# Activation-table loads, first copies and one transposition group moved within a two-block transformer kernel

## What is computed

```
h = rmsnorm(x, g_mix_pre); proj = h @ w_in
y = concat(rmsnorm(forgetting_attention(...)), rmsnorm(chunked_relpos_attention(...)))
x = x + rmsnorm(y @ w_out)
x = x + rmsnorm(memory_cross_attention(rmsnorm(x), rmsnorm(mem), ...))
x = x + rmsnorm(square(relu(rmsnorm(x) @ w_ff1)) @ w_ff2)
proj = rms_norm(x) @ w_in_2            # second block
o_gdn = gated_delta_rule(...) ; o_att = dsa_sparse_attention(...)
x = x + (sigmoid(ga) * o_gdn + sigmoid(gb) * o_att) @ w_out_2
x = x + square(relu(rms_norm(x) @ w_mlp_up)) @ w_mlp_down
```

## Time and profile before

| | |
|---|---|
| median of three runs | 921.76 us |
| the profiled execution | 921.96 us |
| its span | 920.1 us |
| TensorE (matmul) busy | 897.4 us, 98% |
| VectorE busy | 575.2 us, 63% |
| ScalarE busy | 511.8 us, 56% |
| GpSimd busy | 89.6 us, 10% |
| loaded from memory | 147.99 MB |

### The profile page before, as it was taken

The page is one execution under the profiler, slowest core; times in us unless marked ns, Lnnn a source line. Parts: engine busy times, 40 slices in busy tenths (PEclk is TensorE's granted clock), DMA queues, the critical chain, the costliest instruction groups (busy, mean ns, idle before and its releaser), DMA issues.

```text
span 920.1 us, 14611 instructions
## 1 busy us (share of the span) xinstructions
PE 897.4 (98%) x5672; PEld 797.0 (87%) x5672; DVE 575.2 (63%) x899; ACT 511.8 (56%) x932; POOL 89.6 (10%) x111
## 2 busy tenths in 40 slices
PE   6999999999999999999999999999999999999998
PEld 6998977888899998887778989988899799998886
DVE  5455656664676664445656998889846676665333
ACT  4466666664665554335557668787255465554330
POOL 0010000000000000001000412241152101000000
PEclk9999999999999999999999999999999999999999
DMA  9756333464455566555364544454430456555552
GB/s 341 254 183 230 107 124 108 148 226 92 146 175 184 183 207 185 195 202 195 107 214 138 184 139 141 134 164 157 99 143 1 131 190 184 184 183 183 184 189 84
DMA packets 110395, 152.22 MB, mean 165 GB/s; under 512 B 6752, under 2 KB 68344, under 8 KB 109944
## 3 DMA queue, kind: packets, MB, share of 16 engines
q1 hardware_dynamic: 110328, 151.31, 50.7%
HBM read 147.99 MB, written 3.30 MB: 164 GB/s over the span
## 4 chain that ended last, share of the span: by engine, by line
issue 48%; PE 34%; DVE 9%; ACT 4%; POOL 2%; DVEq 1%; DMA 1%; POOLq 1%; ACTq 0%; SPq 0%
PE acc L455 4%; PE acc L469 4%; PE acc L467 4%; PE acc L468 4%; PE acc L457 4%; PE acc L456 4%; DVE s_w_lo L405 3%; ACT s_w_hi L399 1%; PE acc L495 1%; DVE s_qkvT L1522 1%; PE acc L497 1%; PE acc L496 1%; DMA s_w_raw<-in_w_out 1%; ACT s_relu_i L1445 1%; POOL s_rstd L636 1%
## 5 line engine op out<-in xcount | busy, mean ns | idle before, releaser
L405 DVE TENSOR_TENSOR s_w_lo<-s_w_raw,s_w_hi 128x2048 fp32r<-128x2048 f32 (+1 forms) x198 | 312.2, 1594 | 176.5 <-ACT s_w_hi L399 176.2
L399 ACT ACTIVATE s_w_hi<-s_w_raw 128x2048 fp32r<-128x2048 f32 (+1 forms) x198 | 262.7, 1345 | 148.6 <-PE acc L457 102.3
L467 PE MATMUL acc<-s_h_hi,s_w_hi 128*128 128x256 f32 x800 | 229.1, 286 | 0.8 <-DVE s_h_lo L690 0.8
L469 PE MATMUL acc<-s_h_hi,s_w_lo 128*128 128x256 f32 x800 | 227.3, 284 | 0.0
L468 PE MATMUL acc<-s_h_lo,s_w_hi 128*128 128x256 f32 x800 | 227.3, 284 | 0.0
L467 PEld LDWEIGHTS acc<-s_h_hi,s_w_hi 128*128 128x128 f32 x800 | 154.5, 193 | 1.6 <-issue 1.2
L468 PEld LDWEIGHTS acc<-s_h_lo,s_w_hi 128*128 128x128 f32 x800 | 154.6, 193 | 0.3
L469 PEld LDWEIGHTS acc<-s_h_hi,s_w_lo 128*128 128x128 f32 x800 | 154.4, 193 | 0.0
L457 PE MATMUL acc<-s_w_hi,s_hid_lo 128*128 128x512 f32 x224 | 88.3, 394 | 0.0
L456 PE MATMUL acc<-s_w_lo,s_hid_hi 128*128 128x512 f32 x224 | 87.8, 392 | 0.0
L455 PE MATMUL acc<-s_w_hi,s_hid_hi 128*128 128x512 f32 x224 | 86.9, 388 | 0.0
(11 more groups left out here) (323 smaller groups left out, 1429.1 us busy)
## 6 DMA issues: line engine op xcount, KB each, us to landing
s_w_raw<-in_w_in SPq DMA_DIRECT2D x43, 1024.0 KB, 5.2
s_w_raw<-in_w_ff SPq DMA_DIRECT2D x32, 1024.0 KB, 5.2
s_w_raw<-in_w_mlp_up SPq DMA_DIRECT2D x16, 1024.0 KB, 5.5
s_w_raw<-in_w_mlp_down SPq DMA_DIRECT2D x16, 1024.0 KB, 5.0
s_w_raw<-in_w_out SPq DMA_DIRECT2D x8, 1024.0 KB, 5.1
s_w_raw<-in_w_mk SPq DMA_DIRECT2D x4, 1024.0 KB, 5.4
s_w_raw<-in_w_mv SPq DMA_DIRECT2D x4, 1024.0 KB, 5.0
s_w_raw<-in_w_mq SPq DMA_DIRECT2D x4, 1024.0 KB, 5.0
```

What stands on the lines that cost most here:

```text
L399: act.activation(w_hi[u % SPLIT_SLOTS][:, cs], w_raw[u % RAW_SLOTS][:, cs], ACT.Copy).then_inc(w_hi_done, 4 if q is None else 1)
L405: dve.tensor_tensor(w_lo[u % RAW_SLOTS][:, cs], w_raw[u % RAW_SLOTS][:, cs], w_hi[u % SPLIT_SLOTS][:, cs].bitcast(F32), ALU.subtract).then ...
L467: pe.matmul(o, wh[:, cs], hi[:, k, :], start=k == 0, stop=False)
L469: i = pe.matmul(o, wl[:, cs], hi[:, k, :], start=False, stop=k == KC - 1)
```

## The change

Five edits, all of them of the order of work; one new tile of one column and one new activation, used twice.

1. At the start, ScalarE splits quarters 0 and 1 of the first unit, copies banks 0 and 1 to h_hi, splits quarters 2 and 3, and copies banks 2 and 3.
2. Ahead of the evacuation of the second cv unit, ScalarE runs an exponential of one column into the tile `spare`.
3. The gate's activations of the second block stand one unit earlier: behind the first iq unit and no longer behind the first aq unit.
4. Ahead of the evacuation of the second aq unit, the exponential of one column again.
5. Of the five transposition groups behind k = 5, the fifth (the keys) stands behind k = 6, on TensorE and on ScalarE.

```diff
+        spare = sb("spare", [P, 1])
...
-        def nt_act(act, n, hi):
-            for j in range(4):
+        def nt_act(act, n, hi, banks=range(4)):
+            for j in banks:
...
+        def exp_table(act):
+
+            act.activation(spare[:], minus1[:], ACT.Exp)
...
-        def aqk_pe(pe):
-            for j in range(5):
+        def aqk_pe(pe, groups):
+            for j in groups:
...
-        def aqk_act(act):
-            for j in range(5):
+        def aqk_act(act, groups):
+            for j in groups:
...
-            for q in range(4):
+            for q in (0, 1):
                 unit_hi(act, 0, q)
             act.wait_ge(gain_in, 16)
-            nt_act(act, "mix", h_hi)
+            nt_act(act, "mix", h_hi, (0, 1))
+            for q in (2, 3):
+                unit_hi(act, 0, q)
+            nt_act(act, "mix", h_hi, (2, 3))
...
-            for j in range(2):
-                act_unit(act, "cv", j)
+            act_unit(act, "cv", 0)
+            advance_hi(act, of["cv"][1])
+            exp_table(act)
+            evacuate(act, "cv", 1)
...
             act_unit(act, "iq", 0)
+            gates2_act(act)
             act_unit(act, "iq", 1)
             ik_act(act)
             act_unit(act, "aq", 0)
-            gates2_act(act)
             idx_tr_act(act)
-            act_unit(act, "aq", 1)
+            advance_hi(act, of["aq"][1])
+            exp_table(act)
+            evacuate(act, "aq", 1)
             gates2_act_eg(act)
...
                 if k == 5:
-                    aqk_act(act)
+                    aqk_act(act, range(4))
+                if k == 6:
+                    aqk_act(act, (4,))
...
                 if k == 5:
-                    aqk_pe(pe)
+                    aqk_pe(pe, range(4))
+                if k == 6:
+                    aqk_pe(pe, (4,))
```

## The result

The kernel after took 925.13 us (median of ten executions, 923.31 to 925.42), the kernel before 922.4 us beside it (921.55 to 922.78). The ratio is 1.0027, 95% interval 1.0019 to 1.0035: slower by about 2.5 us, where 2.6 us of gain were forecast. The profiled execution of after took 925.12 us, with a span of 923.3 us.

What follows compares the result with a forecast made beforehand. TensorE, busy 897.4 of 920.1 us, was taken as the bound, so only its waits could be won. 0.30 + 1.04 + 0.43 + 0.86 + 0 = 2.63 us gave 919.1 us; stated range 918.0 to 921.3, from part bounds 918.5 to 920.2.

Steps and rivals of the forecast that it cites:

- The 0.08 us added to each idle: Each printed TensorE idle was priced 0.08 us higher, halfway between 0 and 0.16, because matmuls overlap.
- no row prices that, and I take 0: The new 4-byte tile shifts later tiles' addresses; taken as 0 us because all transfers keep their sizes.
- Part 1: Start: earlier h_hi copies let TensorE start 0.59 us earlier, of which 0.30 us is kept, bounds 0 and 0.6.
- the cap: Fourth unit, 31.39: its weights' landing time stays, so TensorE can be at most 0.3 us earlier from there.
- Part 2: First attention: earlier exponential table load removes the 0.96 us wait at the transposes; 1.04 us, bounds 0.9 and 1.1.
- Part 3: Gate: activations one unit earlier remove the 0.35 us wait of its transposes; 0.43 us, bounds 0 and 0.5.
- Part 4: Index scores: earlier exponential table load removes TensorE's 0.78 us wait for the relus; 0.86 us, bounds 0.7 and 1.0.
- Part 5: Fifth group: the 0.77 us wait at 530.49 goes, but the wait at 547.7 grows; 0 us, bounds 0 and 0.85.
- the last part counts: Rival, 8%: VectorE's chain up to 547.7 has hidden slack, so 0.85 us more is won, giving 918.3.
- the loads stay: Rival, 12%: table loads stay on the path or another wait replaces them; parts 2 and 4 worth nothing, 921.0.
- the start or the gate turn against the change: Rival, 8%: the start or the gate's move loses 0.3 to 0.7 us, giving 919.8 to 920.3.
- The fourth: Rival, 7%: slower, as TensorE's clock falls before 547.7 after the idle there grows from 0.90 to about 1.7 us.

Runs made afterwards that it cites:

- e1: The kernel before with the new one-column tile declared and never used; 4.4 us slower.
- e2: The changed kernel with the dummy exponential written into a free column of stat and no new tile; 920.56 us, 0.9983.
- e6: The kernel before with 32 unused bytes just ahead of hid_hi, so that only the hid tiles move; 925.52 us, 1.0033.
- e3: As e2, with the fifth transposition group back behind k = 5, so edits 1 to 4 without the tile; 919.44 us, 0.9971.
- e7: The kernel before with 32 unused bytes just ahead of m_hi, so that only m_hi and m_lo move; 922.91 us, 1.0006.
- e9: As e3, with VectorE's third product of q, k, v moved from ahead of the last attention's first masks to behind them; 918.63 us, 0.9961.
- e4: The kernel before with only the fifth transposition group moved behind k = 6; 922.68 us, 1.0005.
- e5: The changed kernel with the new tile 64 bytes wide, so that later tiles move by 64 bytes and not 32; 920.32 us, 0.9977.
- e10: As e3, with 64 unused bytes ahead of h_hi and 64 behind h_lo; 922.35 us, 1.0003.
- e13: As e9, with 384 unused bytes ahead of h_hi and 128 behind h_lo (h at 0 within 256 bytes); 919.39 us, 0.9969.
- e16: The kernel before with the unused bytes of e14 and none of the edits of order; 910.97 us, 0.9887.
- e17: The kernel before with 64 unused bytes ahead of all its tiles, so that no distance between tiles changes; 922.55 us, 1.0005.
- e18: As e14, with 192 unused bytes ahead of h_hi, 256 fewer; 905.89 us, 0.9829.
- e14: As e12, with 64 unused bytes ahead of hid_hi (hid at 128 within 256 bytes); 907.76 us, 0.9841.
- e20: The kernel before with 192 unused bytes ahead of the weight tiles and 64 behind, moving only weights 64 bytes earlier within 256; 919.84 us, 0.9975.
- e12: As e9, with 448 unused bytes ahead of h_hi and 64 behind h_lo (h at 64 within 256 bytes); 914.57 us, 0.9914.
- e19: The kernel before with 64 unused bytes ahead of the weight tiles and 192 behind, moving only weights 64 bytes later within 256; 921.75 us, 1.0.

## Why the prediction was wrong

**What bounds the kernel: half right.** TensorE does run back to back, with 22.7 us idle in the trace of before. "A change that adds or removes no matmul can only win such moments" is the sentence that fell: the rhythm of hid's matmuls went from 228.9 to 233.4 ns, and 4.5 ns on 768 of them is 3.5 us. The 0.08 us added to each idle, for a change of line, lies where the trace of before has it: a matmul of h or m starts 0.16 us before the modelled end of the one ahead, the scores of L775 behind such a matmul 0.07 before it in 16 of 25 places (101.71, behind one of 0.28 us at 101.51) and 0.16 in the others.

**The step that failed** is the one about the new tile, "no row prices that, and I take 0". It stood at 0 without a bound, and it cost 4.4 us by itself (e1), and 4.1 between e2 and after by their ratios. Of that, 3.0 to 3.5 is hid (e6; the shifts in after say 1.50 + 1.61) and about 0.8 m. In the trace of e1 another 0.7 us is a clock fall at 437.6, behind a wait of 1.06 us; its four other executions had the full clock and lost as much, so the fall is no part of the 4.4. This term alone turned the sign: with it away the same kernel is at 920.56, inside the range.

**Part 1** (0.30): the cap came as worked out, the worth is not shown. The first matmul came 0.38 us earlier and not 0.59, and TensorE now waits 0.89 us for w_lo of the fourth unit at 31.22. The shift there is 0.16 in after and 0.30 in e3, but e1 and e7, which lack the edit, start the unit 0.34 and 0.50 earlier than before too, right behind w_lo. In them the spacing of 0.22 us at the start ends at 14.5 and 14.9 us, in before at 16.6, so TensorE stands at the cap without the edit. What part 1 is worth depends on the execution, and its agreement in e3 is partly luck.

**Part 2** (1.04): right, 0.85 in after and 0.93 in e3. The load stands at 84.34 as named, and the transposes start without a wait at 89.65. **Part 3** (0.43): right, 0.51. **Part 4** (0.86): right, 0.86 in after and 0.84 in e3. The load and the dummy stand at 473.87 and 475.17. At 84.34 the load takes 1.28 us and the dummy starts at 85.64, 0.02 behind it; at 473.87 and 475.17 it is the same. The transposes behind were not late. The trace of before has five loads, each of 1.28 us: at 54.45 and 466.85 in front of a Ln, at 88.43 and 477.15 in front of the first Exp behind it, and at 0.72 in front of the first Square, so that one Square does have a load. None stands between Exp and Tanh. Relu occurs only where the last load was one for Exp.

**Part 5** (0): right in the place and wrong in what follows. The chain of VectorE up to 547.7 held (its pauses there in the trace of before are 25 gaps of 0.07 to 0.09 us between its own instructions, 0.35 at 510.02 for ScalarE's w_hi, and 0.18 at 546.91), the wait grew from 0.90 to 1.87 as forecast (about 1.7), and e9, which shortened that chain, moved it by 0.53. But the growth has a price that 0 to 0.85 left out, the clock. I gave it 7%. It came in all four traces with that idle (after, e2, e4, e5), for 1.31 us in after, and seven of the ten executions of after had less than the full clock, though not always for this wait. My size for it, 2.2 to 4.2 us, and with it 921.3 as the upper end of the range, was an estimate from the start of the trace of before, where matmuls stand 0.22 us apart and not 0.12, taken over 4.8 and 9.3 us. No run shows a fall of that size, nor that the start is one: the granted clock printed for 11.73 to 16.50 us is 1.00. The runs showed a granted clock of 0.50 and a slow stretch of about 2.5 us instead. That is a mis-sized term, and its chance was too low: the only evidence against it was idles of up to 1.06 us in one execution, the new idle was known to be longer, and the same idle of 1.06 us let the clock fall in seven of the 19 traces.

**Sum and rivals.** Parts 1 to 4 alone (e3) give 919.44 us against 922.16 in the same comparison, 2.72 us (interval 1.8 to 3.6), where the sum said 2.63. The rivals that the last part counts, that the loads stay and that the start or the gate turn against the change did not come true. The fourth came true in that the clock fell, for 1.31 us; the rest of the loss was none of them.

**What stays open.** Why the spacings go with the distance between operands is not shown, nor do the traces print a place: the distances are estimates from the sizes. Nor is it shown what chooses between 113.3 and 117.8 ns at distance 192, nor why the clock fell at 427 to 438 us in seven traces (e1, e2, e10, e13, e16, e17, e18) and not in the twelve others behind the same wait. In after and e6 TensorE also waits 0.41 and 0.31 us for x near 735, which it does not in before; no run tells why.

## What to carry to other kernels

Here an unused tile of 4 bytes (e1) took hid's matmuls from 228.9 to 233.3 ns and the kernel 4.4 us up, with no wait between them and no printed duration to tell of it; the page's busy time hinted at it, 901.0 for 897.4 us in after. So when a change adds, removes or resizes a tile, compare the start-to-start spacing of the same matmuls before and after, and test the layout by an unused tile, which is a change of one line. A gain by edits of the order is to be judged with the layout held fixed (here a free column of an existing tile did it). And the longer wait of TensorE was not free though the scores behind it started no later (1.87 us for 0.90, 547.60 for 547.72): the granted clock was 0.50 behind it, which cost 1.31 us. The granted clock of each execution tells how often it fell: in seven of the ten of after.

## What the runs showed of the hardware

- A tile of 4 bytes (after, e1) and a pad of 32 (e6 for hid, e7 for m) have the same effect here: 45 matmuls of hid take 10.50 us for 10.30, 24 instructions with m 2.80 for 2.74.
- The spacing of this kernel's fp32r matmuls at a granted clock of 1.00 went with the distance of the operands modulo 256 bytes, as estimated from the sizes: 226.7 (distance 0: e5, e14, e16, e18, e20) to 233.4 ns (224: after) for 512 columns, 113.3 (192: e14, e16, e18) to 120.0 ns (0: before) for 256. At distance 192 the 256-column form has two rhythms, 113.3 and 117.8 (e16, at 31 us). The padding of e16 is worth 11 us of 922, in a kernel whose TensorE is busy 98%.
- TensorE's granted clock fell to 0.50 behind all four traced idles of 1.83 to 1.88 us (after, e2, e4, e5, at 545 to 548), and behind the idle of 1.06 us at 427 to 438 in seven traces of 19; it stayed at 1.00 behind idles of 1.25 to 1.45 us in e12, e14, e16, e18 and e19. In e1_tile_only (0.50 from 438.2 to 440.3) the 512-column matmuls stood 0.43 us apart there. TensorE's rows:

```profile
437.62 0.74 PE L496 MATMUL acc<-s_w_hi,s_h_hi 128*128 128x512 f32 x1 [1.06 <-DVE s_h_lo L716]
...
439.01 0.63 PE L496 MATMUL acc<-s_w_hi,s_h_hi 128*128 128x512 f32 x1
439.44 0.63 PE L497 MATMUL acc<-s_w_lo,s_h_hi 128*128 128x512 f32 x1
```
